# The first modulation unit of a two-block stack split between TensorE's products and VectorE's chunk sums

## What is computed

```
c_act = silu(c)
mod = (c_act @ ada_w[i] + ada_b[i]).reshape(bsz, N_SUB, 3, d)
shift, scale, gate = mod[:, :, 0], mod[:, :, 1], mod[:, :, 2]
h = rms_norm(x, g) * (1 + scale) + shift        # adaln
x = x + gate * sublayer(h)                      # the feed-forward ones with half the gate
swiglu(h) = (silu(h @ w_a) * (h @ w_b)) @ w_out # d_ff = 2816
```

## Time and profile before

| | us |
|---|---|
| median of 3 runs (lowest, highest) | 3392.11 (3378.27, 3396.86) |
| the profiled execution, its own time | 3389.97 |
| its span in the trace | 3388.3 |
| PE busy in the span | 3231.6 (95%) |
| DVE busy | 2281.1 (67%) |
| ACT busy | 1299.9 (38%) |
| first product of the first network starts at | 68.94 |

### The profile page before, as it was taken

One profiled execution on the slowest core, in us unless ns is written; L12 is line 12 of the kernel. 1 busy time (PEld: TensorE's weight loads), 2 busy tenths in 40 slices (PEclk: granted clock), 3 DMA queues, 4 the chain that ended last, 5 costly groups with the idle time before them and its releaser, 6 DMA issues.

```text
span 3388.3 us, 52394 instructions
## 1 busy us (share of the span) xinstructions
PE 3231.6 (95%) x20804; PEld 2831.3 (84%) x20804; DVE 2281.1 (67%) x3155; ACT 1299.9 (38%) x1962; POOL 93.6 (3%) x180
## 2 busy tenths in 40 slices
PE   7998998899999999999999999999989999999898
PEld 6996778799898887998987898986688898968797
DVE  2877855587886874878766877876652766642465
ACT  2444021244545662444443444443121444432343
POOL 0000000000000000000000000000000000000000
PEclk9999997899999999999998999999998999999999
DMA  7763422476674524766644765742300553443353
GB/s 294 282 238 141 156 79 73 159 281 232 239 258 166 183 106 177 281 240 233 249 175 153 278 242 205 266 181 85 115 1 12 194 186 131 168 149 118 142 188 142
DMA packets 68750, 609.71 MB, mean 180 GB/s; under 512 B 7632, under 2 KB 7664, under 8 KB 30320
## 3 DMA queue, kind: packets, MB, share of 16 engines
q1 hardware_dynamic: 42912, 466.90, 37.2%
q0 software_dynamic: 25344, 138.42, 11.7%
q10 hardware_dynamic: 336, 2.13, 0.2%
HBM read 605.33 MB, written 2.10 MB: 179 GB/s over the span
## 4 chain that ended last, share of the span: by engine, by line
PE 83%; DVE 11%; ACT 3%; issue 2%; DMA 1%; SPq 0%; DVEq 0%; POOLq 0%; ACTq 0%
PE psum L283 31%; PE psum L687 21%; PE psum L711 17%; PE psum L689 11%; PE psum L281 2%; DVE arena L613 1%; DMA ada_in<-in_ada_w 1%; DVE ada_sum L445 1%; DVE norm_pair L598 1%; PE psum L1336 1%; DVE arena L1962 1%; ACT up_part L663 1%; PE psum L1387 1%; DVE wkv_base L1734 1%; DVE small L1733 1%
## 5 line engine op out<-in xcount | busy, mean ns | idle before, releaser
L687 PE MATMUL psum<-h_part,up_part 128*128 128x512 f32 x3168 | 1138.0, 401 | 23.7 <-DVE h_part L605 16.7
L689 PE MATMUL psum<-h_part,up_part 128*128 128x256 f32 x3168 | 893.8, 282 | 0.0
L687 PEld LDWEIGHTS psum<-h_part,up_part 128*128 128x128 f32 x3168 | 600.4, 190 | 167.4 <-issue 19.1
L689 PEld LDWEIGHTS psum<-h_part,up_part 128*128 128x128 f32 x3168 | 603.6, 191 | 0.0
L711 PE MATMUL psum<-hidden_part,down_part 128*128 128x256 f32 x4752 | 601.0, 283 | 0.0
L711 PEld LDWEIGHTS psum<-hidden_part,down_part 128*128 128x128 f32 x4752 | 582.9, 190 | 8.9
L672 DVE TENSOR_TENSOR up_part<-weights,up_part 128x2048 fp32r<-128x2048 f32 x198 | 453.3, 2289 | 135.7 <-ACT up_part L663 135.2
L283 PE MATMUL psum<-arena,weights 128*128 128x256 f32 (+5 forms) x1936 | 420.5, 382 | 11.1 <-DVE arena L1633 7.5
L283 PEld LDWEIGHTS psum<-arena,weights 128*128 128x128 f32 (+4 forms) x1936 | 330.3, 193 | 94.9 <-issue 40.1
L663 ACT ACTIVATE up_part<-weights 128x2048 fp32r<-128x2048 f32 x198 | 376.8, 1903 | 42.4 <-DMA weights<-in_weights 41.5
L793 DVE TENSOR_REDUCE arena<-psum 128x256 f32<-128x512 f32 x396 | 267.3, 687 | 132.7 <-PE psum L689 132.4
(11 more groups left out here) (269 smaller groups left out, 2531.5 us busy)
## 6 DMA issues: line engine op xcount, KB each, us to landing
weights<-in_weights SPq DMA_DIRECT2D x294, 1536.0 KB, 6.5
ada_in<-in_ada_w POOLq DMA_DIRECT2D x176, 768.0 KB, 4.9
consts<-in_consts SPq DMA_DIRECT2D x1, 1848.0 KB, 9.5
x<-in_x SPq DMA_DIRECT2D x1, 1024.0 KB, 5.5
v_first<-arena ACTq DMA_DIRECT2D x1, 1024.0 KB, 5.8
arena<-v_first ACTq DMA_DIRECT2D x1, 1024.0 KB, 4.8
out<-x SPq DMA_DIRECT2D x1, 1024.0 KB, 3.9
params<-in_params SPq DMA_DIRECT2D x1, 458.0 KB, 3.1
```

Of the source, the lines that this page charges most:

```text
L687: mm(k.psum[:, bank, :].rearrange("p (i t) -> p i t", i=2), lhsT=k.up_part[0][:, j % 2, b:b + P], rhs=k.h_parts[:, :, t], start=t == 0, st ...
L689: ins = mm(k.psum[:, bank, 0:T], lhsT=k.up_part[1][:, j % 2, b:b + P], rhs=k.h_part[0][:, t], start=False, stop=t == KT - 1, skip_group_ch ...
```

## The change

The first sublayer's `ada_w` is cut in two. Its first 1536 columns stay in weight slots, now slots 0 to 3 instead of 0 to 7, and are multiplied on PE as before (96 products). Its other 1536 columns come as eight chunks at the head of POOL's stream; DVE sums them (`open_ada_sum`) and PE adds them with 12 products by `pick`, as for later sublayers. The params have a semaphore of their own and are loaded first, then the three slots, then x and consts. The sum of squares (`norm_sums`) goes to bank 5 and stands between PE's product 72 and 73, and the root and the reciprocal move ahead with it; `norm_products` returns at once for the first sublayer. All network slots have numbers lower by four (n0 = 4 for the first).

```
 def stream_weights(k, sp, w, slots):
-    for n in range(RING):
-        sp.dma_start(k.weights[:, n], w[n]).then_inc(k.weights_loaded[n], 16)
     with sp.Fori(1, slots // RING) as g:
...
-    chunks = units * ADA_STEPS
+    chunks = ADA_OPEN + units * ADA_STEPS
...
+def open_ada_sum(k, dve, t):
+    out, buf, c = k.ada_sum[:, ADA_CHUNK:], k.ada_in[:, t % 2], k.c_act[:, t:t + 1]
+    dve.wait_ge(k.ada_loaded[t % 2], 16 * (t // 2 + 1))
+    if t == 0:
+        ins = k.nc.vector.tensor_scalar(out, buf, c, None, ALU.mult)
+    else:
+        dve.wait_ge(k.sem["ada_summed"], t)
+        ins = k.nc.vector.scalar_tensor_tensor(out, buf, c, out, ALU.mult, ALU.add)
+    ins.then_inc(k.sem["ada_summed"], 1)
...
     pe.wait_ge(k.sem["c_ready"], 1)
-    for m in range(24):
+    for m in range(12):
+        if m == 9:
+            pe.wait_ge(k.sem["inputs_loaded"], 32)
+            norm_sums(k, pe, pr, 0)
         for t in range(KT):
-            pr.mm(k.psum[0:24, 3, 256:384], k.c_pick[:, t, 23 - m:47 - m], pr.take(), (m, t) == (0, 0),
-                  (m, t) == (23, KT - 1), k.sem["mod_rows"] if (m, t) == (23, KT - 1) else None)
+            pr.mm(k.psum[0:24, 3, 256:384], k.c_pick[:, t, 23 - m:47 - m], pr.take(), (m, t) == (0, 0), False)
+    pe.wait_ge(k.sem["ada_summed"], ADA_OPEN)
+    for m in range(12, 24):
+        pr.mm(k.psum[0:24, 3, 256:384], k.const("pick")[:, 23 - m:47 - m], k.ada_sum[:, m * P:(m + 1) * P],
+              False, m == 23, k.sem["mod_rows"] if m == 23 else None)
     turn_mod_rows(k, pe, pr, 0)
...
+    if n == 0:
+        norm_root(k, act, n)
     if ffn is not None and not follows(n):
         up_high(k, act, ffn, 0, 0)
...
-    norm_root(k, act, n)
+    if n:
+        norm_root(k, act, n)
...
 def norm_products(k, pe, pr, n):
+    if n == 0:
+        return
...
-    return 5 if n < NORMS and SUBS[n - 1] != "ffn" else 3
+    return 5 if n == 0 or n < NORMS and SUBS[n - 1] != "ffn" else 3
...
-    slot, q, ffns, mixers, out = 8, 0, 0, 0, []
+    slot, q, ffns, mixers, out = 4, 0, 0, 0, []
...
-            sp.dma_start(k.params[:, :], params).then_inc(sem["inputs_loaded"], 16)
+            sp.dma_start(k.params[:, :], params).then_inc(sem["params_loaded"], 16)
+            for n in range(RING):
+                sp.dma_start(k.weights[:, n], w[n]).then_inc(k.weights_loaded[n], 16)
             sp.dma_start(k.x[:, :, :], x_in).then_inc(sem["inputs_loaded"], 16)
             sp.dma_start(k.consts[:, :], consts).then_inc(sem["inputs_loaded"], 16)
...
-            dve.wait_ge(sem["inputs_loaded"], 48)
+            dve.wait_ge(sem["params_loaded"], 16)
+            for t in range(KT - 1):
+                open_ada_sum(k, dve, t)
+            norm_reciprocal(k, dve, own, 0)
+            open_ada_sum(k, dve, KT - 1)
+            up_low(k, dve, 0, 0, 0)
+            dve.wait_ge(sem["inputs_loaded"], 32)
             mod_vector(k, dve, own, 0)
...
             pr = Products(k, pe)
-            pe.wait_ge(sem["inputs_loaded"], 48)
             first_mod_products(k, pe, pr)
             pr.align()
```

More of the change, by code:

```diff
@@ L35 @@
 ADA_STEPS = 2 * KT
+ADA_OPEN = KT
 FFN_SLOTS = FT
@@ L79, in weight_slots @@
 def weight_slots(v):
-    out = [slots_of([blocks_of(v["ada_w"][0][:, :ADA_COLS])])]
+    out = [slots_of([blocks_of(v["ada_w"][0][:, :ADA_CHUNK])])]
     for i in range(DEPTH):
@@ L372, in layout @@
     k.ada_loaded = [ctx.enter_context(nc.semaphore(f"ada_loaded{r}")) for r in range(2)]
-    for n in ("weights_used", "inputs_loaded", "c_ready", "ada_summed", "mod_summed",
+    for n in ("weights_used", "params_loaded", "inputs_loaded", "c_ready", "ada_summed", "mod_summed",
               "mod_rows", "mod_rows_read", "c_silu",
@@ L435, in ada_sum @@
         return
-    n, half = (unit - 1) * ADA_STEPS + i, i % 2
+    n, half = ADA_OPEN + (unit - 1) * ADA_STEPS + i, i % 2
     out, buf = k.ada_sum[:, half * ADA_CHUNK:(half + 1) * ADA_CHUNK], k.ada_in[:, half]
@@ L480, in mod_sums @@
 def mod_sums(k, pe, pr, u):
-    pe.wait_ge(k.sem["ada_summed"], ADA_STEPS * u)
+    pe.wait_ge(k.sem["ada_summed"], ADA_OPEN + ADA_STEPS * u)
     pe.wait_ge(k.sem["mod_ready"], u)
@@ L573, in norm_act, with norm_sums @@
             .then_inc(sem["h_ready"], 1)
-def norm_products(k, pe, pr, n):
-    if n < NORMS:
-        pe.wait_ge(k.sem["mod_ready"], n + 1)
+def norm_sums(k, pe, pr, n):
     for t in range(KT):
@@ L582, in norm_products @@
               k.sem["mean_square"] if t == KT - 1 else None)
+def norm_products(k, pe, pr, n):
+    if n == 0:
+        return
+    if n < NORMS:
+        pe.wait_ge(k.sem["mod_ready"], n + 1)
+    norm_sums(k, pe, pr, n)
     if early_mod(n):
@@ L586, in norm_products, with norm_reciprocal @@
             turn_mod_rows(k, pe, pr, n + 1)
+def norm_reciprocal(k, dve, own, n):
+    dve.wait_ge(k.sem["rms_ready"], n + 1)
+    own.of(k.nc.vector.reciprocal(k.rstd[:, :], k.rms[:, :]))
 def norm_vector(k, dve, own, n, gain, src=None, signal="scaled", ffn=None, shift=None, parts=None):
     src = k.x if src is None else src
-    if ffn is not None and not follows(n):
+    if n and ffn is not None and not follows(n):
         up_low(k, dve, ffn, 0, 0)
@@ L594, in norm_vector @@
         parts.low(dve, 0)
-    dve.wait_ge(k.sem["rms_ready"], n + 1)
     if n < NORMS:
         dve.wait_ge(k.sem["mod_ready"], n + 1)
-    own.of(k.nc.vector.reciprocal(k.rstd[:, :], k.rms[:, :]))
+    if n:
+        norm_reciprocal(k, dve, own, n)
     def low(t):
@@ L3025, in _ @@
             ev = Evacuation(k, act)
-            act.wait_ge(sem["inputs_loaded"], 48)
+            act.wait_ge(sem["params_loaded"], 16)
             nc.scalar.activation(k.c_act[:, :], k.param("c", 0, KT), ACT.Silu).then_inc(sem["c_silu"], 1)
+            act.wait_ge(sem["inputs_loaded"], 32)
             for u, (kind, n, slot, q, m) in enumerate(subs):
@@ L3105 @@
         "weights": weight_slots(v),
-        "ada_w": ada[ADA_STEPS:],
+        "ada_w": np.concatenate([ada[1:ADA_STEPS:2], ada[ADA_STEPS:]]),
         "consts": np.concatenate(list(CONST_PARTS.values()), 1),
```

## The result

The changed kernel takes 3461.04 us (median of four, 3447.98 to 3466.15), the kernel before 3391.02. The ratio is 1.0197, with a 95% interval of 1.0175 to 1.0219: slower by 59 to 74 us. The profiled execution took 3457.36 us, 67.4 more than the one before. The forecast was 3454, with a range of 3442 to 3480.

A forecast was written before the change was run, and what follows sets the result against it. PE bounds the kernel, and time is won or lost only where it waits. From the profiled 3389.97 us, the opening's gain of 9, the late release's loss of 71.3 and 1.4 for the clock give 3454, range 3442 to 3480.

The forecast's parts named there:

- The two large terms of the sum: Opening: a gain of 9 us; first network's twenty steps with late loads: a loss of 71.3 us.
- The late release decides: First network: slot 3 stays uncounted, so weight loads of pieces 2 to 21 come one step late; loss 71.3 us.
- The step of 11.9: First network: issue 0.16, landing 6.3, about 0.05 and 5.37 to the next L786 make each step 11.9 us, before 8.53.
- down(j)'s own wait: First network: down(j) waits for D(j+1), the next piece's end of L786, instead of D(j); no separate size given.
- The opening, a gain of 9: Before the first network: last chunk sum ends at 50.9, first product near 60 instead of 68.94.
- The clock, 1.4 at the end: End of the first network: PE at half clock after the last idle 3.4 us costs 2.8; half taken, 1.4 us.
- The sum: Whole execution: 3389.97 - 9 + 71.3 + 1.4 = 3453.7, so 3454 us.
- A count paid elsewhere: Rival, first network: an overlooked instruction counts slot 3 in time, only the opening's gain shows; 3381 us, chance 0.08.
- Late landings: Rival, first network: loads land in 7.4 us, not 6.3, making steps of 13.0 and 3476 us; chance 0.09.
- The clock as the bound: Rival, first network: PE bursts wholly at half clock need 17.1 us, more than a step; 3558 us, chance 0.05.

The follow-up runs named there:

- e1_pay: The changed kernel plus one `align` ahead of the 12 products by `pick`, so the first of them counts slot 3 as used; 3384.74 us.
- e2_before_debt: The kernel before, with the eight products of the first sublayer's sum of squares issued without the account, opening untouched; 3469.50 us.
- e4_down_early: The changed kernel with down(j) of the first network waiting for a count lower by one, loads still one step late; 3455.89 us.
- e5_down_late: e1_pay with down(j) of the first network waiting for a count higher by one, loads in time; 3391.77 us.
- e9_norm_behind: e1_pay with sum of squares, root and reciprocal put back behind the modulation; ratio 0.9998 against the kernel before.
- e6_six_chunks: e1_pay with six chunks in place of eight, the rows of the last two multiplied on PE; 3377.18 us.

## Why the prediction was right, point by point

The mechanism came as foretold. The two large terms of the sum were each about 3 us off, both in the same direction.

- *The late release decides.* Shown: e1_pay takes the loss away by paying the count, e2_before_debt makes it without the rest of the change.
- *The step of 11.9.* Issue 0.18, landing 6.3, and 5.37 from ACT's start to the end of the next L817 came as foretold; the first step took 11.84. The mean of the twenty, (313.47 - 72.61) / 20, is 12.04. The landings between 86 and 310 us were 6.3 in the median, but one took 8.1:

```profile
DMA to landing us min/median/max: 6.1/6.3/8.1
```

  The loss of the twenty steps is 74.2, not 71.3. Of the 2.9 us between, that one load, issued at 144.23, makes 1.9 (ACT's part starts 8.20 behind its issue). No chunk delayed it: from 144 to 152.5 us the queue q0 moved no packet, and no chunk was issued between 137.25 and 174.92. What did is open.
- *down(j)'s own wait is not the bound.* Shown by e4_down_early and e5_down_late.
- *The opening, a gain of 9.* It was 5.56: the term was mis-sized. The last sum ended at 54.7, not 50.9. Chunk 2, issued at 17.07, was summed only from 29.27, some 12 us of landing where 5.5 a chunk had been taken as the pace, and POOL issued its loads 0.7 us behind a sum instead of at once. The pick products took 5.31 at half rate (5.1 taken; the row that this was read from, 24 records in the kernel's first 5 us of products, has PEclk 1.00 beside it, so it was no evidence for the lower clock, and that the size fits is luck), the rest 3.32 from their end to the first product (3.4 taken). That the norm part alone brings the gain, which the prediction's sum implied, e9_norm_behind showed.
- *The clock, 1.4 at the end.* None of it came: from down(19) to the second sublayer it takes 20.69 us, before 20.58. The idle in front of down(19) was only 1.66.
- *The sum.* -5.6 + 74.2 = 68.6, against 68.75 in the traces; predicted were -9 + 71.3 + 1.4 = 63.7. The opening was 3.4 and the steps 2.9 us worse than foretold, the clock's 1.4 didn't come: 5 us in all. The rest of the execution was 1.3 us shorter, so the profiled one missed 3453.7 by 3.7 us and the median of four missed 3454 by 7.
- *The rivals.* A count paid elsewhere: no. Late landings: one of 8.1, the other nineteen 6.1 to 6.7; with all of them the steps lost 2.9 us more than forecast, not 22. The clock as the bound: no, for the reason given: the burst behind a long wait stayed far under a step. But PE did not stand 3.4 us in every step, it alternated between about 1.6 and 3.4 (below).

## What to carry to other kernels

Where an increment is carried by "the next instruction of this kind", moving or removing an instruction moves the increment; look who pays after every reorder. The price of a release that comes one step late isn't the delay of the release: once issue, landing and the preparation behind it (here 0.2 + 6.3 + 5.4 us) exceed a step, that chain becomes the step. And two halves of a change can each be worth nothing alone: here the early norm gained nothing beside a full PE stream, and the split that made PE idle gave nothing until something filled it.

## What the runs showed of the hardware

PE's clock followed the idle time within the first network in a pattern of two steps. A row here reads: stretch, its length, PE's busy time (instructions), PEclk, DMA share, GB/s. The changed kernel around the down products at 108.34:

```profile
104.00:108.00 4.00, 1.10 (x7) 0.99 0.21 86
108.00:110.00 2.00, 1.66 (x7) 0.50 0.34 74
110.00:112.00 2.00, 2.00 (x13) 0.67 0.91 362
112.00:118.00 6.00, 6.00 (x38) 1.00 0.68 251
```

After idle times of 3.2 to 3.6 us the 24 products took 4.4 to 4.6 us and the clock was at 0.50 of 2.4 GHz, its lower level of 1.2; the burst then ended later, the next idle time was only 1.5 to 1.7 us, and the products behind that took 3.1 us at full clock. One of the short ones went the other way, with PEclk at 0.50 from 146 to 148 us:

```profile
144.11 4.47 PE L742 MATMUL psum<-hidden_part,down_part 128*128 128x256 f32 x24 [1.73 <-DVE down_part L817]
```

In e5_down_late an idle time of 2.69 us was followed by 4.61 us too. In the opening, after 14.52 us of idle time, the pick products of the changed kernel ran wholly at the lower level:

```profile
54.00:60.00 6.00, 5.25 (x24) 0.50 0.46 152
```

In e6_six_chunks, after 3.10 us, the same twelve took 2.80 us, which is the full rate, and PEclk stayed at 1.00 from 45 to 53 us; so an idle time of about 3 us went both ways in these runs. The Trainium skill (TensorE: Matmul & The Clock Gate, Part 1) says that an idle PE falls back to the lower clock and that how much runs at it varies between runs of one kernel. The traces agree with the first. Each kernel has only one trace here, but in four kernels with the same opening the twelve pick products took 4.47 to 5.31 us after idle times of 12.8 to 14.5 us. What decided in each case stays open.

The first six chunks of the changed kernel's opening, issued while q1 was moving slots, x or consts, landed 8.4 to 14.5 us after their issue, the last two after 4.6; those issued between 84 and 290 us took 4.3 to 6.4. That a third buffer would shorten the opening was not tried.
